# Sliding-window attention in a single-core transformer kernel: P transposed in 32x32 blocks by VectorE, PV on four row quarters of TensorE, the scaling of P on GpSimd, and the output projection's columns taken by turns

## The reference

```python
q, k = rms_norm_2(q, q_norm), rms_norm_2(k, k_norm)    # over each head's 64
q, k = apply_rope(q, cos, sin), apply_rope(k, cos, sin)
scores = einsum('bnqhgd,bnkhd->bnhgqk', q, k_window) * 64 ** -0.5
scores = where(valid, scores, -inf)          # blocks of 128 queries, window of 128 keys back
m = maximum(max(scores), sink); p = exp(scores - m)
probs = p / (sum(p) + exp(sink - m))
out = einsum('bnhgqk,bnkhd->bnqhgd', probs, v_window)
x = x + out.reshape(b, s, 32 * 64) @ w_o
```

## Time and profile before

| | |
|---|---|
| time, median of 3 runs | 1921.42 us (1920.27 to 1923.04) |
| time of the profiled execution | 1922.04 us, of which 1920.2 is the span of the profile |
| TensorE matmuls busy | 1910.9 us, 100% of the span |
| VectorE busy | 1295.5 us, 67% |
| ScalarE busy | 1081.3 us, 56% |
| GpSimd busy | 557.4 us, 29% |
| TensorE's granted clock | 9 tenths or more in each of 40 slices |

### The profile page before, as it was taken

The page is one execution under the profiler, slowest core; times in us unless marked ns, Lnnn a source line. Parts: engine busy times, 40 slices in busy tenths (PEclk is TensorE's granted clock), DMA queues, the critical chain, the costliest instruction groups (busy, mean ns, idle before and its releaser), DMA issues.

```text
span 1920.2 us, 28392 instructions
## 1 busy us (share of the span) xinstructions
PE 1910.9 (100%) x10592; PEld 1566.4 (82%) x10592; DVE 1295.5 (67%) x1852; ACT 1081.3 (56%) x1441; POOL 557.4 (29%) x616
## 2 busy tenths in 40 slices
PE   9999999999999999999999999999999999999999
PEld 7888878888887788888887778888888888888887
DVE  5899967556879888887658877555555555544443
ACT  7444466546868686875467865544444444443332
POOL 1899852306060514202401006022222222220000
PEclk9999999999999999999999999999999999999999
DMA  9666656566555555555664445666666666656664
GB/s 321 190 189 184 182 167 198 177 208 181 162 172 167 166 166 154 177 164 168 194 200 138 129 139 190 194 195 190 195 194 189 196 191 193 195 193 192 195 193 159
DMA packets 183168, 352.64 MB, mean 184 GB/s; under 512 B 11792, under 2 KB 12304, under 8 KB 183056
## 3 DMA queue, kind: packets, MB, share of 16 engines
q1 hardware_dynamic: 182912, 351.12, 59.9%
q10 hardware_dynamic: 144, 0.01, 0.0%
HBM read 348.99 MB, written 2.10 MB: 183 GB/s over the span
## 4 chain that ended last, share of the span: by engine, by line
PE 93%; DVE 2%; ACT 1%; POOL 1%; issue 1%; DVEq 1%; DMA 0%; POOLq 0%; SPq 0%; ACTq 0%
PE acc L552 30%; PE acc L554 29%; PE acc L553 29%; PE T L664 1%; PE T L511 1%; DVE w_lo L1190 1%; PE T L759 1%; DVEq L1176 1%; POOL kb L469 1%; PE T L748 1%; POOL kf L469 0%; ACT w_hi L801 0%; PE T L655 0%; DMA raw<-in_conv_w_in_dram 0%; PE T L736 0%
## 5 line engine op out<-in xcount | busy, mean ns | idle before, releaser
L1190 DVE TENSOR_TENSOR w_lo<-raw,w_hi 128x1024 fp32r<-128x1024 f32 x568 | 698.9, 1233 | 539.0 <-ACT w_hi L801 530.7
L801 ACT ACTIVATE w_hi<-raw 128x1024 fp32r<-128x1024 f32 x656 | 688.7, 1057 | 597.7 <-PE acc L554 577.5
L552 PE MATMUL acc<-w_hi,h_hi 128*128 128x512 f32 x1884 | 742.5, 394 | 1.0 <-DVE w_lo L1190 0.9
L553 PE MATMUL acc<-w_lo,h_hi 128*128 128x512 f32 x1884 | 733.5, 389 | 2.3 <-issue 2.3
L554 PE MATMUL acc<-w_hi,h_lo 128*128 128x512 f32 x1884 | 734.1, 390 | 0.0
L552 PEld LDWEIGHTS acc<-w_hi,h_hi 128*128 128x128 f32 x1884 | 353.7, 188 | 80.3 <-issue 5.6
L554 PEld LDWEIGHTS acc<-w_hi,h_lo 128*128 128x128 f32 x1884 | 353.7, 188 | 77.2 <-issue 2.5
L553 PEld LDWEIGHTS acc<-w_lo,h_hi 128*128 128x128 f32 x1884 | 354.0, 188 | 71.1
L500 POOL COPY fT<-fq 32x256 f32<-32x256 f32 x176 | 110.8, 630 | 388.2 <-DVE fq L1652 381.3
L438 POOL TENSOR_TENSOR w_lo<-raw,w_hi 128x1024 fp32r<-128x1024 f32 x80 | 190.4, 2407 | 71.8 <-ACT w_hi L801 71.7
L1270 DVE SCALAR_TENSOR_TENSOR T<-vpad,feat,T 128x256 f32<-128x256 f32 x464 | 182.4, 478 | 0.0
(11 more groups left out here) (244 smaller groups left out, 1548.2 us busy)
## 6 DMA issues: line engine op xcount, KB each, us to landing
raw<-in_hgrn_w_in_dram SPq DMA_DIRECT2D x160, 512.0 KB, 3.7
raw<-in_conv_w_in_dram SPq DMA_DIRECT2D x96, 512.0 KB, 4.2
raw<-in_ffn_w_gate_dram SPq DMA_DIRECT2D x88, 512.0 KB, 4.3
raw<-in_ffn_w_up_dram SPq DMA_DIRECT2D x88, 512.0 KB, 4.3
raw<-in_ffn_w_down_dram SPq DMA_DIRECT2D x88, 512.0 KB, 4.5
raw<-in_attn_w_qkv_dram SPq DMA_DIRECT2D x40, 512.0 KB, 3.8
raw<-in_conv_w_out_dram SPq DMA_DIRECT2D x32, 512.0 KB, 3.8
raw<-in_hgrn_w_out_dram SPq DMA_DIRECT2D x32, 512.0 KB, 4.6
```

The lines of the kernel that those rows point to most:

```text
L552: nc.tensor.matmul(o, hi[:, kt, a], w_hi[:, slot, kk, :], start=kt == 0, stop=False)
L553: nc.tensor.matmul(o, hi[:, kt, a], w_lo[:, slot, kk, :], start=False, stop=False)
L801: A(w_hi[:, slot, :, :], raw[:, slot, :, :], ACT.Copy).then_inc(hi_ready, 1)
L1190: TT(w_lo[:, slot, :, :], raw[:, slot, :, :], rounded(w_hi[:, slot, :, :]), ALU.subtract).then_inc(split_ready, 1)
```

## The change

**TensorE.** `turn_p` and ScalarE's `p_copy` go. VectorE transposes P instead (`p_turn`), in one operation per head that turns 32x32 blocks in place. A product with V then takes 32 keys at a time: `mix_v(g)` is one step per group with 60 matmuls of 32 rows, 64 stationary columns and 128 moving columns, where row quarter a works into PSUM bank a and even and odd heads into the two column halves. It stands at e+16 (before: four steps at e+9 to e+12). V is laid out for that once, by 16 copies of GpSimd (`v_rows`).

**GpSimd.** It scales P (`scale_p`, two operations per head pair), raises the queries' mean squares to the power -1/2 (`q_power`, a 128x16 operation; before, root and reciprocal), and takes the w_lo of three chunks in eight instead of two.

**Moved.** ScalarE's `q_out` is one chunk earlier (e+3), the squares are at e+5; VectorE's `rope` is at e+4, `sums` at e+6. y is taken out once per group (`y_out_hi` at e+20, `y_low` at e+21).

**att_out by turns.** Rows 0 to 1023 of w_o are used first for all four column groups, then rows 1024 to 2047 again for all four: eight segments of four chunks. x is therefore added to twice per column group; the four additions in between are the new `first_part`. At the norm behind it, column group 2 too is now transposed by TensorE, and `late` goes.

The core of the diff:

```diff
-    return 24 <= i < 50 and i % 8 < 2
+    return 23 <= i < 50 and i % 8 in (7, 0, 1)
...
+        if per_iter == 2 * columns:
+            self.seq = [(p * columns + k, c) for p in range(2) for ks, cs in (((0, 1), (0, 1)), ((0, 1), (2, 3)), ((2,), range(4)), ((3,), range(4)))
+                        for k in ks for c in cs]
...
+            def v_rows():
+                pool.wait_ge(a_ev, 1)
+                pool.wait_ge(a_T, 1)
+                for a in range(4):
+                    for b in range(4):
+                        nc.gpsimd.tensor_copy(vrows[a * QUARTER:(a + 1) * QUARTER, b::4, :], kvtok[b * QUARTER:(b + 1) * QUARTER, :, KVH * HD:])
+                nc.gpsimd.drain().then_inc(a_rows, 1)
+
+            def scale_p(g, i):
+                pool.wait_ge(a_inv, 4 * g + i + 1)
+                for tb in range(TB):
+                    p, inv = sm[:, 2 * i:2 * i + 2, (1 + tb) * P:2 * (1 + tb) * P], ast[:, 6, 8 * tb + 2 * i:8 * tb + 2 * i + 2]
+                    last = nc.gpsimd.tensor_tensor(p, p, inv.unsqueeze(2).to_broadcast([P, 2, (1 + tb) * P]), ALU.mult)
+                last.then_inc(a_n, 1)
+
+            def q_power(g):
+                nc.gpsimd.drain()
+                pool.wait_ge(a_ss, g + 2)
+                nc.gpsimd.tensor_tensor(ast[:, 8, :], ast[:, 1, :], halves[:, :], ALU.pow).then_inc(a_std, 1)
...
+            v_rows()
+            q_power(0)
             for n in range(ph["kv_q"].chunk0, ph["att_out"].chunk1):
                 if low_by_pool(ph, n):
...
+                    i = n - ph["kv_q"].chunk0
+                    if i % 8 == 1:
+                        for p in range(4):
+                            scale_p(i // 8 - 3, p)
+                        if i < 49:
+                            q_power(i // 8 - 2)
...
-            def mix_v(g, i):
+            def mix_v(g):
+                pe.wait_ge(a_rows, 1)
+                pe.wait_ge(a_pt, 4 * g + 4)
+                pe.wait_ge(a_sm, 8 * (min(g + 1, 3) + 1))
...
+                for tb in range(TB):
+                    for step in range(5):
+                        for a in range(4):
+                            blocks = range(4 + a, 4 + a + 5) if tb else range(a + 1)
...
+                            for c in range(2):
+                                o = T[c * HD:(c + 1) * HD, a, :].rearrange("p (i t q) -> p i t q", t=TB, q=QUARTER)[:, 0:4, tb, :]
+                                w = PT[r, c:8:2, b * QUARTER:(b + 1) * QUARTER]
+                                last = nc.tensor.matmul(o, vrows[r, key, g * HD:(g + 1) * HD], w, start=step == 0, stop=step == len(blocks) - 1)
...
+            def first_part(name, k):
+                dve.wait_ge(chunk_used, ph[name].done(0, k))
...
+                    if ph[name].in_parts:
+                        at.put(ph[name].last[k] + 3, lambda k=k: first_part(name, k))
```

More of the change, by code:

```diff
@@ L108, in done, with first_reads @@
         return self.base(j) + self.last[k] + 1
+    def first_reads(self, k):
+        return k == 0 or self.in_parts and k == self.columns
     def use(self, j, k):
@@ L444, in x_moves @@
             def x_moves(s):
[L445 removed]
+                for k in range(on_tensor(s)):
                     pool.wait_ge(n_q, 3 * (s - 1) + k + 1)
[L447 to L449 removed]
+                    if s < 3 and k:
                         pool.wait_ge(n_lo, 4 * (s - 1) + k)
@@ L542, in stream @@
                         continue
-                    if need is not None and k == 0:
-                        need(c)
+                    row = p.row(k, c)
+                    if need is not None and p.first_reads(k):
+                        need(row)
                     if c == 0 and not (isinstance(p.use(j, k), int) and p.use(j, k) == 0):
@@ L565, in x_turn, with step @@
             def x_turn(name, s, free):
-                def step():
-                    pe.wait_ge(x_done, 4 * s)
+                def step(k):
+                    pe.wait_ge(x_done, 4 * (s - 1) + k + 1)
                     pe.wait_ge(*free)
-                    transposes(T01, x[:, :, group_columns(3)], n_T)
-                return Hooks().put(ph[name].end(3) + 2, step).later(32)
+                    transposes(T01 if k == 3 else T23, x[:, :, group_columns(k)], n_T)
+                at = Hooks()
+                for k in range(on_tensor(s), 4):
+                    at.put(ph[name].end(k) + 2, lambda k=k: step(k))
+                return at
             def normed(s):
@@ L1621, in y_low, with p_turn @@
-            def y_low(g, b):
-                dve.wait_ge(a_hi, 2 * g + b + 1)
-                kk = slice(4 * g + 2 * b, 4 * g + 2 * b + 2)
-                low(flat(hy_lo[:, kk, :]), T[:, 2 + b, :], flat(y_hi[:, kk, :]), a_lo)
+                V.reciprocal(inv, l).then_inc(a_inv, 1)
+            def p_turn(g, i):
+                dve.wait_ge(a_n, 4 * g + i + 1)
+                if g:
+                    dve.wait_ge(a_o, g)
+                else:
+                    dve.wait_ge(a_rows, 1)
+                for h in (2 * i, 2 * i + 1):
+                    last = V.transpose(PT[:, h, :], sm[:, h, P:4 * P])
+                last.then_inc(a_pt, 1)
@@ L1634, in _ @@
-                    for b in range(2):
-                        at.put(e + 14 + b, lambda g=g, b=b: y_low(g, b))
+                        at.put(e + 9 + i, lambda g=g, i=i: inverse(g, i))
+                    for i in range(4):
+                        at.put(e + (11, 13, 14, 15)[i], lambda g=g, i=i: p_turn(g, i))
+                    at.put(e + 21, lambda g=g: y_low(g))
             stream("kv_q", 0, x_norm("hgrn_out", 2).later(32).with_(at))
```

190 lines of the change are left out of this document (97 added, 93 removed).

## The result

The changed kernel takes 1925.72 us (median of 20 runs, 1923.31 to 1929.37), the kernel before 1921.22 (20 runs, 1920.06 to 1923.04). The ratio is 1.0022, with a 95% interval of 1.0016 to 1.0028: slower by 4.5 us. The profiled execution took 1928.37, so it lies 2.65 above its kernel's median; its span is 1926.6, against 1920.2 before.

A forecast was written before the change was run, and what follows sets the result against it. The prediction took TensorE to bound the kernel before, and the loop over the queries' 1/rms to set the new round. Work -15.3 plus waits 19.8 (12.5 + 4.1 + 3.2) gave +4.5: 1926.0 us, range 1917.5 to 1932.

The forecast's parts named there:

- TensorE's work, -15.3: TensorE in attention and norm: steps removed -25.6, four new PV bursts +9.4, eight extra transposes +0.9, net -15.3 us.
- the 0.6 us more a burst: PV bursts: estimate from the Trainium skill's 3.1-times gain for four row tiles; four bursts 2.5 us longer.
- The bound of +17: PV bursts: if only column halves overlap, 6.6 us of products per group, 17 us more in all.
- the 0.36 around a burst: TensorE: time around a burst beyond its products, read from scores and included in the 2.34 us PV burst.
- The loop over the queries' 1/rms: Mask to next group's mask through all engines: 31.1 us against TensorE's 28.6; waits 12.5 us in all, bounds 6 and 17.
- the 0.7: Loop: addition per group for GpSimd and VectorE operations lengthening each other, between 0 and 1.5 us.
- The 2.1 for group 0: Wait in group 0, whose power stands behind GpSimd's 16 v_rows copies, 11.7 us in all; 2.1 taken between 0 and 3.5.
- 1 us less per round is 4 us: Remark against the main forecast: power, y_low and handovers are estimates; each 1 us off a round changes the time by 4.
- Rival 2: Loop closes in time if the power costs 1.6 instead of 2.9 without clashes: 1914 to 1918 us, chance 0.15.
- Chunk 48: att_out's third column group waits for first_part(0), behind mask and maxima in VectorE's list: 4.1 us, 3 to 5.
- The norm: Norm behind att_out: GpSimd's copies delay group 1's splits, so chunks 73 and 74 wait 3.2 us, 0 to 6.
- Rival 4: TensorE: waits of 4 us lower its clock, one to three chunks each 2.75 longer: 1929 to 1935 us, chance 0.07.

The follow-up runs named there:

- experiment 10: Changed kernel with the 60 products of a PV burst issued one row quarter after the other, not by turns: 1931.75 us (one run).
- experiment 3: Changed kernel with the squares one chunk earlier on ScalarE and their sum directly behind the rotation on VectorE: 1926.75 us, 1.0021 of the kernel before.
- experiment 5: Changed kernel with the sum of squares one w_lo behind the rotation and the last inversion of P's sums ahead of it: 1932.54 us, 1.0052 of the kernel before.
- experiment 11: Changed kernel with GpSimd's power replaced by a product of the same 128x16 operands (queries then wrongly scaled): 1924.93 us, 1.0014 of the kernel before.
- experiment 9: Changed kernel with first_part, y_low, sums, inversions and P's first transposes reordered, norm buffer added and group 2 split later, fourth w_lo on GpSimd: 1915.37 us, 0.9962 of before.
- experiment 1: Changed kernel with each first_part one chunk earlier in VectorE's list: 1919.78 us, 0.9986 of the kernel before.
- experiment 2: Changed kernel with column group 1 of the norm behind att_out transposed into a buffer of its own: 1924.81 us, 1.0013 of the kernel before.

## Why the prediction was right, point by point

- **TensorE's work, -15.3:** right in each term (2.37 for 2.34 a burst, 0.87 for 0.9). The assumption that four row quarters by two column halves run at once is borne out, as long as they alternate in the list (experiment 10); the 0.6 us more a burst that stood beside it as an estimate did not come. The bound of +17 leaves out the 0.36 around a burst: by the prediction's own terms it is 4 x (6.6 + 0.36 - 2.34) = 18.5.
- **The loop over the queries' 1/rms:** its length was forecast at 31.1, or 31.8 with clashes, and was 30.5, 31.3 and 31.9. The power was 2.9, as taken. How TensorE takes the lateness was less exact: 12.5 forecast, 8.6 stood (0.6, 4.3, 1.2, 2.5). Clashes of VectorE with GpSimd's scaling on the path cost 1.0 in the round of group 1 (w_lo 1.76 and 1.68 instead of 1.2) and 0.55 in those of groups 2 and 3 (1.75), near the 0.7; so the links without them came to a little less than 31.1. The 2.1 for group 0 had the wrong reason: `v_rows` took 16 us, more than the 11.7 forecast, but ended 2.5 us before the sum that the power waits for, so it was not in the way. And the price "1 us less per round is 4 us" could not be cashed: experiments 3, 5 and 11 shortened or moved a link and the rounds stayed, since another link took its place. Only experiment 9, with several links at once, shortened them, by 0.5 to 1.1 us.
- **Rival 2 (the loop closes in time if the power is short)** was worked out wrong for that reason. With a power of 0.22, more than the rival asked for, TensorE's waits in the loop hardly change, and the kernel stays slower than before. Its number did not fit its condition either: 19.8 - 8 = 11.8 us of waits are more than the 11.5 below which the prediction calls the kernel faster.
- **Chunk 48:** the mechanism is right (experiment 1). Two details of its text are not: the pair is full after chunk 45, not 41, and the w_lo that chunk 47 needs is GpSimd's, not VectorE's. The size is 5.2 for 4.1 in the profiled execution, where L1670 was held up by 1.7, and 4.2 in that of experiment 2, where it was not.
- **The norm:** 2.5 for 3.2, at chunks 73 and 74, for the reason given: GpSimd's copies. They took 8.9 and 11.8, against 9 to 12 forecast. Column group 0 is full after chunk 61, not 59.
- **Rival 4 (the clock)** should have been a term of the sum. It was given a chance of 0.07, and in the profiled execution it is 5.5 us of the 21.8. The forecast of the sum, 19.8, came near because too much standing and no clock offset each other (-3.5, +5.5). On the medians the forecast of +4.5 met +4.5; by the profiled execution it is 2 us short. So the size was luck in part. And so was the sign: without the clock the account is -15.3 + 16.3 = +1.0, which the prediction itself would call no change. The places of the waits were right, and so were the reasons, but for group 0.

The clock also goes with most of the spread of the times, by the mean granted clock of each execution. Of the 71 executions of the kernel before beside the experiments, the 37 at 1.000 took 1919.8 to 1922.5 us and the 34 at 0.999 took 1922.5 to 1924.0; a place for such a step is the stand in hgrn, which is followed by the lower clock in 11 of the 14 traces and not in that of the kernel before. Of the 20 of the changed kernel, the four at 0.998 took 1923.3 to 1923.8, the sixteen at 0.995 to 0.997 1924.5 to 1929.4.

What stays open: what decides whether the lower clock follows a stand of 2.4 to 3.4 us, and which link sets the round once one has been taken out. Not tried: the sinks copied by ScalarE, or ahead of the wait for the power, so that GpSimd's w_lo can't hold the mask up. Experiment 11 makes that the next link to try; that it would give time is not shown.

## What to carry to other kernels

Work taken from the bounding engine pays in full only if the round through the other engines is shorter than its new round; count that loop from end to end before the change. When it is longer, look for waits that are not part of it (here one number at chunk 48 was worth 7 us), since taking one link out of a loop with near rivals gained at most 0.8 us here (1.0022 to 1.0014, within the noise). And price a wait of several us on TensorE with what comes behind it, not with its length alone.

## What the runs showed that I had not expected

- A copy or scaling of 8 numbers per partition on VectorE, 0.17 us alone, takes up to 2.07 us when it starts inside a w_lo of GpSimd (2.4 us); it ends with it. Reductions, 32x32 transposes and operations that read PSUM kept their length in the same place. So a tiny copy on a critical path can cost nearly as much as the GpSimd instruction beside it.
- After TensorE has stood for 2.4 to 7.7 us, its matmuls mostly start 0.43 instead of 0.23 us apart (granted clock 0.50) for the next 3 to 6 us, which costs 1.4 to 2.9 us on top. After stands of up to 2.0 us they never did, and after some of 2.4 to 3.4 neither.
- Float32 products of 32 rows by 64 stationary columns with 128 moving columns cost 0.036 us each by turns over eight tiles (60 in 2.17) and 0.07 when issued quarter by quarter (60 in 4.22).
